# First expert pair of a mixture-of-experts encoder: its rows taken from x on chip, the experts' order formed by two small products

## What is computed

```
glog = xf @ wg_r + bg_r                    # 4 groups
g_idx = argmax(glog)
elog_g = (xf @ we_r + be_r)[group g_idx]   # 8 experts of that group
top_v, top_i = top_k(elog_g, 2)
gate = softmax(top_v) * softmax(glog)[g_idx]
for each chosen expert e of each token x:
    y += gate * ((silu(x @ w_gate[e]) * (x @ w_up[e])) @ w_down[e])
x = x + y;  out = rms_norm(x)
```

## Time and profile before

| | us |
|---|---|
| median of three runs | 1148.36 |
| span of the profiled execution | 1144.7 |
| median less that span | 3.7 |
| PE busy | 1049.2 (92%) |
| DVE busy | 463.5 (40%) |
| POOL busy | 112.9 (10%) |
| HBM over the span | 258 GB/s mean |

### The profile page before, as it was taken

How to read it: one execution, slowest core, us unless ns; L and a number is a source line. 1 busy time by engine, 2 the same in 40 slices (tenths; PEclk the granted TensorE clock), 3 DMA queues, 4 the chain that set the end, 5 groups by cost and what they waited for, 6 DMA issues and landing times.

```text
span 1144.7 us, 11623 instructions
## 1 busy us (share of the span) xinstructions
PE 1049.2 (92%) x4578; PEld 546.0 (48%) x4578; DVE 463.5 (40%) x780; ACT 186.8 (16%) x487; POOL 112.9 (10%) x169
## 2 busy tenths in 40 slices
PE   6999999999999999999999999997877789987885
PEld 3577744555444546777657433332332233333331
DVE  3259734573665025003325764332323233332235
ACT  0147133433112300112201010000000000000001
POOL 1200001132105101000000110000000000000002
PEclk9999999999999999999999899998999899999999
DMA  8611140222230733113055899999999999999997
GB/s 258 239 57 39 53 152 1 81 109 83 74 111 30 255 147 117 56 50 147 1 216 230 306 395 421 429 425 427 427 426 427 430 424 427 426 426 426 424 410 257
DMA packets 56983, 281.50 MB, mean 246 GB/s; under 512 B 13333, under 2 KB 15253, under 8 KB 44130
## 3 DMA queue, kind: packets, MB, share of 16 engines
q1 hardware_dynamic: 44882, 262.57, 57.2%
q10 hardware_dynamic: 7152, 8.96, 2.2%
q0 software_dynamic: 4896, 9.23, 2.2%
HBM read 272.82 MB, written 22.81 MB: 258 GB/s over the span
## 4 chain that ended last, share of the span: by engine, by line
PE 70%; DMA 17%; DVE 5%; SPq 5%; issue 2%; ACT 0%; DVEq 0%; POOL 0%; ACTq 0%; POOLq 0%
PE banks L517 23%; DMA arena<-in_exp_w_down_dram 14%; PE banks L505 14%; PE banks L915 10%; PE banks L905 6%; SPq L1159 4%; PE banks L521 3%; DMA arena<-expert_rows 2%; PE banks L767 2%; PE score_pair L741 2%; PE banks L655 1%; DVE arena L1769 1%; PE score_pair L571 1%; PE banks L872 1%; PE banks L605 1%
## 5 line engine op out<-in xcount | busy, mean ns | idle before, releaser
L517 PE MATMUL banks<-arena 128*128 128x512 f32 x640 | 285.6, 600 | 2.5 <-DMA arena<-in_w_in_dram 1.8
L915 PE MATMUL banks<-arena 128*64 128x512 f32 x1024 | 236.1, 617 | 36.9 <-issue 34.8
L517 PEld LDWEIGHTS banks<-arena 128*128 128x128 f32 x640 | 120.0, 192 | 147.2 <-issue 145.7
L915 PEld LDWEIGHTS banks<-arena 128*64 128x64 f32 x1024 | 83.2, 142 | 186.1 <-issue 184.8
L505 PE MATMUL banks<-arena 128*128 128x288 f32 x640 | 156.1, 406 | 0.0
L905 PE MATMUL banks<-arena 128*64 128x512 f32 x512 | 116.4, 608 | 23.8 <-DMA arena<-in_exp_w_down_dram 15.9
L505 PEld LDWEIGHTS banks<-arena 128*128 128x128 f32 x640 | 121.4, 190 | 33.8 <-issue 0.4
L1384 ACT ACTIVATE arena<-banks 128x512 f32<-128x512 f32 (+6 forms) x135 | 61.6, 492 | 377.3 <-PE banks L517 111.0
L905 PEld LDWEIGHTS banks<-arena 128*64 128x64 f32 x512 | 38.2, 140 | 90.8 <-issue 76.3
L1607 ACT ACTIVATE arena<-banks,arena 128x512 f32<-128x512 f32 x17 | 11.7, 687 | 411.4 <-PE banks L915 387.7
L2159 DVE SCALAR_TENSOR_TENSOR arena<-banks,arena 128x512 f32<-128x512 f32 x34 | 25.4, 750 | 102.8 <-PE banks L905 95.2
(11 more groups left out here) (320 smaller groups left out, 965.1 us busy)
## 6 DMA issues: line engine op xcount, KB each, us to landing
arena<-in_exp_w_gate_dram SPq DMA_DIRECT2D x30, 2048.0 KB, 32.3
arena<-in_exp_w_up_dram SPq DMA_DIRECT2D x29, 2048.0 KB, 32.9
arena<-in_exp_w_down_dram SPq DMA_DIRECT2D x28, 2048.0 KB, 35.3
arena<-in_w_in_dram SPq DMA_DIRECT2D x7, 2048.0 KB, 8.5
arena<-in_exp_w_down_dram SPq DMA_DIRECT2D x16, 512.0 KB, 11.1
expert_rows<-arena SPq DMA_DIRECT2D x4, 1152.0 KB, 8.0
out_dram<-arena SPq DMA_DIRECT2D x4, 1024.0 KB, 10.5
arena<-in_w_mem_k_dram SPq DMA_DIRECT2D x2, 2048.0 KB, 9.7
```

The lines of the kernel that those rows point to most:

```text
L517: ins = mm(b[:, :], x, w[:, k, :], start=k == 0, stop=k == KC - 1)
L915: ins = mm(bank[own, :], xgT[:, k, own], w[j][:, k, :], start=k == 0, stop=k == KC - 1)
```

## The change

Pass 0 no longer takes its rows from the gather. While tiles 3 and 4 are still being chosen, PE multiplies x (which is still in SBUF) by the one-hots of pass 0: per tile eight matmuls of 128 x 128 (`first_rows`), accumulated over the five tiles in the two banks `pair`. The result is already transposed. DVE copies it with the gain into a new buffer xgT0. These 40 matmuls replace `keep_running` (9 matmuls of 128 x 512) and pass 0's `turn_rows`.

The list product for tiles 3 and 4 (`last_near_tokens`) moves into the gate product of pass 0, before its fifth step; the read of the lists by DVE, and so both gathers, move behind DVE's whole list arithmetic. The up product of pass 0 waits until DVE has read the list, since both use banks[1]. Gather 0 is still made, because ACT and DVE need the rows of x for the sum, and ACT now waits for it.

The experts' order was a comparison of 32 x 32 in every partition, a product and a sum, three DVE operations of 1024 elements. It is now two small products on PE: one that turns the positions into a column (L896 of the kernel after), one that sums (L901, between the first and second step of the gate product), with two short DVE operations.

The late half of slot 9 waits for the first tile's `first_rows` instead of the gather.

```diff
@@ PE
             pe.wait_ge(near_hot, 2)
-            near_list = A.open(pe)[:, 0:4]
+            near_list = banks[1][:, 0:4]
+            def first_rows(t, half):
+                rows = TILES[t][1]
+                x = x_sb[0:rows, t, :].rearrange("p (d k) -> p k d", k=KC)
+                for k in range(4 * half, 4 * half + 4):
+                    ins = mm(pair[:, half, (k % 4) * P:(k % 4 + 1) * P], x[:, k, :], near_hots[0:rows, t, 0, :],
+                             start=t == 0 and k % 4 == 0, stop=t == SAMPLE, skip_group_check=True)
+                return ins
             near_tokens(0, 3)
-            pe.wait_ge(a_free, A.filled)
-            keep_running(3)
+            pe.wait_ge(lg_read, NT)
+            for t in range(2):
+                for half in range(2):
+                    ins = first_rows(t, half)
+                if t == 0:
+                    ins.then_inc(x_placed, 1)
             pe.wait_ge(sel_ready, 3)
             ranks(3, NT)
+            for half in range(2):
+                first_rows(2, half)
             pe.wait_ge(near_hot, 3)
-            near_tokens(3, NT).then_inc(near_full, 1)
-            pe.wait_ge(a_free, A.filled)
-            keep_running(6)
+            for half in range(2):
+                first_rows(3, half)
+                first_rows(SAMPLE, half).then_inc(SP_.tx_full, 1)
             pe.wait_ge(v_free, V.filled)
             pe.wait_ge(a_free, A.filled)
+            pe.wait_ge(order_in, 1)
+            mm(banks[2][0:NE, 0:1], pos[0:1, :], ones[0:1, 0:1], start=True, stop=True).then_inc(order_out, 1)
...
+                    if k == 1 and quarter_read is not None:
+                        order_sums()
+                    if k == 4 and quarter_read is not None:
+                        last_near_tokens()
...
-            pe.wait_ge(xg_ld[0], 16)
-            turn_rows(SP_, xg_rows[0])
...
+                    if i == 0:
+                        pe.wait_ge(near_std, 1)
@@ SP
-            sp.wait_ge(xg_ld[0], 16)
+            sp.wait_ge(x_placed, 1)
@@ ACT
                     act.wait_ge(table_ready, 1)
+                    act.wait_ge(xg_ld[0], 16)
@@ DVE
             near_rows(3, NT)
-            ve.wait_ge(near_full, 1)
-            listed = A.banks[mark["near"]][:, 0:4].rearrange("p (i v) -> p v i", v=2)
-            ts(near_row, listed[:, 0], float(NOROW), None, ALU.add).then_inc(near_ready, 1)
...
-            copy_rows(SP_, 0)
-            n.link(tt(order_cmp, pos.unsqueeze(1).broadcast_to([P, NE, NE]), wide(iota32, NE), ALU.is_equal))
-            n.link(tt(order_cmp, order_cmp, per_tile(iota32, NE), ALU.mult))
-            n.link(red(tmp32, order_cmp, AX_X, ALU.add))
-            v.tensor_copy(order_i, tmp32).then_inc(order_ready, 1)
+            copy_half(SP_, 0, 0, xgT0)
+            ve.wait_ge(order_out, 1)
+            ts(tmp32[0:NE, :], iota32[0:NE, :], banks[2][0:NE, 0:1], tokv[0:NE, 0:1], ALU.is_equal, ALU.mult).then_inc(order_in, 1)
+            copy_half(SP_, 0, 1, xgT0)
+            ve.wait_ge(order_out, 2)
+            ts(order_i[0:1, :], banks[2][0:1, NE:2 * NE], float(NOROW), None, ALU.add).then_inc(order_ready, 1)
...
+            ve.wait_ge(near_full, 1)
+            listed = banks[1][:, 0:4].rearrange("p (i v) -> p v i", v=2)
+            ts(near_row, listed[:, 0], float(NOROW), None, ALU.add).then_inc(near_ready, 1)
```

More of the change, by code:

```diff
@@ L864, in _, with order_sums, last_near_tokens @@
             pe.wait_ge(near_hot, 2)
-            near_list = A.open(pe)[:, 0:4]
[L866 to L872, removed]
-            near_tokens(0, 3)
-            pe.wait_ge(a_free, A.filled)
-            keep_running(3)
+            near_list = banks[1][:, 0:4]
[6 more added lines that the diff above has]
+                return ins
+            near_tokens(0, 3)
+            pe.wait_ge(lg_read, NT)
[4 more added lines that the diff above has]
+                    ins.then_inc(x_placed, 1)
             pe.wait_ge(sel_ready, 3)
             ranks(3, NT)
+            for half in range(2):
+                first_rows(2, half)
             pe.wait_ge(near_hot, 3)
-            near_tokens(3, NT).then_inc(near_full, 1)
-            pe.wait_ge(a_free, A.filled)
-            keep_running(6)
+            for half in range(2):
+                first_rows(3, half)
+                first_rows(SAMPLE, half).then_inc(SP_.tx_full, 1)
             pe.wait_ge(v_free, V.filled)
             pe.wait_ge(a_free, A.filled)
+            pe.wait_ge(order_in, 1)
+            mm(banks[2][0:NE, 0:1], pos[0:1, :], ones[0:1, 0:1], start=True, stop=True).then_inc(order_out, 1)
+            def order_sums():
+                pe.wait_ge(order_in, 2)
+                mm(banks[2][0:1, NE:2 * NE], ones[0:NE, 0:1], tmp32[0:NE, :], start=True, stop=True).then_inc(order_out, 1)
+            def last_near_tokens():
+                near_tokens(3, NT).then_inc(near_full, 1)
             def turn_rows(S, rows):
@@ L2073, in _, with copy_half @@
                 n.link(tt(rk32, rk32, tmp32, ALU.add))
+            n.link(tt(pos, others, rk32, ALU.mult))
+            n.link(stt(out=pos, in0=first2[:, 0], scalar=float(2 * OVER_AFTER), in1=pos, op0=ALU.mult, op1=ALU.add))
+            stt(out=pos, in0=first2[:, 1], scalar=float(2 * OVER_AFTER + 1), in1=pos, op0=ALU.mult, op1=ALU.add).then_inc(order_in, 1)
+            ve.wait_ge(order_in, 1)
+            def copy_half(S, n, half, xT):
+                k = slice(4 * half, 4 * half + 4)
+                ve.wait_ge(S.tx_full, 2 * n + half + 1)
+                tt(xT[:, k, :], pair[:, half, :].rearrange("p (k t) -> p k t", k=4),
+                   gain_rows[:, k].unsqueeze(2).broadcast_to([P, 4, P]), ALU.mult).then_inc(S.xT_cp, 1)
             def copy_rows(S, n):
                 for half in range(2):
[L2078 to L2090 removed]
+                    copy_half(S, n, half, xgT)
+            copy_half(SP_, 0, 0, xgT0)
[4 more added lines that the diff above has]
+            ts(order_i[0:1, :], banks[2][0:1, NE:2 * NE], float(NOROW), None, ALU.add).then_inc(order_ready, 1)
             n.link(ts(pos, pos, float(CAP), None, ALU.mult))
```

25 lines of the change are left out of this document (10 added, 15 removed).

## The result

The changed kernel takes 1158.17 us (median of 4 runs, 1155.88 to 1158.85) against 1148.05 us of the kernel before (4 runs, 1147.06 to 1148.55): ratio 1.0088, 95% interval 1.0076 to 1.0100. It is slower by 0.9%. The profiled execution took 1158.85 us with a span of 1157.1, 12.4 us more than the 1144.7 before. The medians differ by 10.1 us only: the profiled execution of the changed kernel was the longest of its four, and the one of before was a short one (more on this behind the experiments).

A forecast was written before the change was run, and what follows sets the result against it. The weight stream, unbroken from about 652 us, was taken to bound the kernel. Early loads 1.2 us earlier, with slack covering PE's 0.6 us gain, gave span 1143.5, plus 3.7 around it: 1147.2 us, range 1145.2 to 1150.0.

The forecast's parts named there:

- any rival of mine: Alternatives: late gather 1149.2 to 1151.6 us (chance 0.16), clock 1148.4 (0.10), more gain 1145.6 (0.18), no effect 1148.4 (0.08).
- The 40 matmuls: `first_rows` on PE before the gate product: 1.8 us per tile at high clock, `ranks` 0.8 us late, the rest hidden.
- rival C: PE idle at 645.5 starts the gate product at half speed, losing 1.7 us there; time 1148.4; chance 0.10.
- A clock of 0.5 in the gate product: Named sign that the forecast is wrong: the gate product running at a granted clock of 0.5.
- the 0.9 saved at `turn_h`: Between up and down product: DVE reaches its hidden values earlier, so 2.6 us instead of 3.5.
- The end as a date of the stream: Kernel end equals when the weight stream runs unbroken plus fixed bytes; the change shifts it by -1.2 us.
- The new wait: PE waits 2.3 us behind the up product for gather 1, issued at 655.6 and landing at 664.1.
- Order and list product: Both small products inside pass 0's gate product lengthen it by 1.15 us, between 0.8 and 1.4.
- The order part at nothing: Removing three 1024-wide DVE operations (3.8 us) beside the gate product gains nothing; two order records on PE take 0.3 us, partly hidden.
- gate product 3.1 us earlier, all but 0.6 taken by the gather: Gate product starts at 646.75; after the wait for gather 1 the down product starts at 666.7 against 667.32.
- the 3.7 us between the profiled span and the median: Added to the forecast span of 1143.5 us as time around it, giving 1147.2.

The follow-up runs named there:

- e2: Changed kernel with first_rows taking 128 neighbouring columns of x instead of every eighth (output not the reference's): 1148.71 us, ratio 1.0007 to the kernel before.
- e5: Changed kernel with neighbouring columns, pass 0's gate and up weights and gain reordered to match, so output is the reference's: 1148.21 us, ratio 1.0004 to the kernel before.
- e1: Kernel before with unread rows of 16 matmuls of various operand strides added at its end: 1204.74 us including those rows.
- e3: Changed kernel with the list product in front of tile 3's rows and DVE reading it behind the first copy: 1156.21 us, ratio 1.0076.
- e4: Kernel before with only the experts' order changed to two small PE products in place of three 1024-wide DVE operations: 1148.22 us, ratio 1.0006.
- e6: e5 with the list product in front of tile 3's rows and its read behind the first copy: 1144.62 us, ratio 0.9976 to the kernel before.
- e7: e6 with half of tile 1's rows moved behind `ranks`: 1145.35 us, ratio 0.9979 to the kernel before.
- e8: e5 with `turn_rows` of pass 1 moved behind pass 0's down product, gathers still late: 1145.89 us, ratio 0.9983 to the kernel before.
- e9: Changed kernel with only `turn_rows` of pass 1 moved behind pass 0's down product: 1155.69 us, ratio 1.0074 to the kernel before.
- e10: e5 with the list product between steps 1 and 2 of the gate product, read by DVE ahead of the list arithmetic: 1145.12 us, ratio 0.9978.

## Why the prediction was wrong

Forecast 1147.2 in a range of 1145.2 to 1150.0; measured 1158.17, far outside, and slower than any rival of mine.

**The step that failed** is the part "*The 40 matmuls*": 1.8 us a tile, 0.8 us of delay for `ranks` and nothing for the rest. I took the price of a record from the earlier trace rows, matmuls of the same shape and type but with neighbouring words as operands, and did not look at the address pattern that the diff itself spells out. Per tile it is 4 us, not 1.8. What hung on that term then went wrong in order:

- Tiles 0 and 1 ended at 642.7, not 639.5, so the positions were ready 2.95 us later than my 645.9, at 648.85.
- The other 48 records, forecast hidden by 645.5, took until 655.5. The gate product started 8.9 us later than forecast: 3.0 from `ranks` (with the offset of 0.74), the rest from these. With neighbouring words it started at 647.10 (e2) and 646.20 (e5), against my 646.75. Less their offsets that is 1.3 us later and 0.3 us earlier than forecast; the two differ in how long the low clock lasted (6.54 and 5.44 us for the same first 32 records).
- Gate and up product took 16.85 us (655.66 to 672.51). In e2, the same instructions took 15.47; the 1.4 us are the half clock at their start. It was rival C in kind, but C saw it behind an idle moment of PE, and here it came behind matmuls that showed no idle time. A clock of 0.5 in the gate product was one of the signs that I had named for being wrong; it stood there for the first 3 us.

**The sum closes** on the date of the loads: gate product 5.8 us later than before (offset included), gate and up 2.9 longer, from there to the down product 1.45 longer (the gather's wait of 2.17 less the 0.9 saved at `turn_h`, and small change), the down product 2.5 longer: 12.7, as in SP's timeline.

**What held.** The end as a date of the stream: 12.7 us at the loads of 674.45 gave 12.4 on the span, at unchanged rates behind 700 us. Over the profiled executions of all variants but e1 it holds within 2 us:

| | loads behind pass 0's down product | span | difference |
|---|---|---|---|
| before | 674.45 | 1144.7 | 470.25 |
| after | 687.12 | 1157.1 | 469.98 |
| e2 | 677.86 | 1147.8 | 469.94 |
| e3 | 683.05 | 1154.7 | 471.65 |
| e4 | 674.79 | 1146.7 | 471.91 |
| e5 | 675.57 | 1145.8 | 470.23 |
| e6 | 672.77 | 1144.1 | 471.33 |
| e7 | 672.57 | 1144.4 | 471.83 |
| e8 | 673.05 | 1144.9 | 471.85 |
| e9 | 683.89 | 1154.1 | 470.21 |
| e10 | 674.26 | 1144.5 | 470.24 |

The differences fall in two groups, near 470.2 and 471.7, and no run shows why. Nor does the table alone tell the stream from PE, since these loads go out when PE ends the down product; that the stream runs full behind them is read from the rates.

The new wait: 2.3 us forecast, 2.17 measured in the changed kernel and 2.83 in e2. In the changed kernel this is partly luck: gather 1 was issued 9.6 us later than forecast (665.22 for 655.6) and the up product ended 10.7 us later (672.51 for 661.85), which nearly cancel. From issue to landing it took 9.4 us there and 9.7 in e2, where I had put 8.5. Order and list product: 1.15 forecast, 1.5 in e2 (15.47 less 13.95). The order part at nothing: e4.

**What else was missed.** Even with the failed term right, the forecast was 1.6 to 2 us too kind (a ratio of 0.9990 against 1.0004 in e5 and 1.0007 in e2). Its path: gate product 3.1 us earlier, all but 0.6 taken by the gather. Not counted was that PE went on at half speed for a while behind the wait: 2.8 us on e2's down product, about 1 us in e5, where it fell on the transposes. And the 3.7 us between the profiled span and the median were not what lies around a span: that is about 1.75 in every run where both are known. The other 1.95 us say that the profiled execution of before was about that much faster than its median (an estimate, since its own time is not on record). Dates of single executions are therefore worth no more than 1 to 2 us against each other; which of e5, e6, e8 and e10 is faster is read from their medians.

An example is e10, which beats e5 by 3.1 us in the median while its loads are only 1.3 us earlier. The two profiled executions differ by 1.3 us in time as well (1147.49 and 1146.22): that of e5 was 0.7 us below its median, that of e10 1.1 above.

**Open.** What makes executions of one kernel differ by 2 to 4 us; the length of the low clock ahead of the gate product is one part that the traces show. Why the down product ran part of its time at half clock in the changed kernel, e2 and e9 and not in e5, e6, e7, e8 and e10. Of the slowdown's parts (late `ranks`, late rows, half clock) each is read from the trace, and only their sum was undone, in e2.

## What to carry to other kernels

Take the price of a matmul from a row with the same strides of both operands, not only the same shape: for the stationary one the width of LDWEIGHTS in ns, 192 against 335, tells the two apart in the trace. A strided moving operand hardly shows there (207 ns, L1062 of e1), only in the time per record. Where a new operand is a view with a step of four words or more and the moving side is narrow, reorder something that is loaded anyway (here the weights' rows, e5). And when an instruction is taken off the path, look at what else was moved with it: here the gathers went back behind the list arithmetic, and PE, in order, gave back all that was gained until they, or the instruction that waits for them, were moved (e6, e8, e10).

## What the runs showed of the hardware

- fp32 matmuls of 128 x 128 against 128 columns, at full clock: 0.117 us a record with neighbouring words, 0.123 with every second, 0.238 with every fourth, 0.243 with every eighth; 0.238 with the moving operand at every eighth. No cost with 512 moving columns (0.435) or in transposes (0.119 and 0.121), one row each.
- At half clock the strided ones take 0.278 us a record (e3, 8.89 us for 32), about a tenth more than the 0.25 at full clock in the changed kernel: halving the clock changes their pace little.
- The granted clock fell to 0.50 while PE was shown 100% busy with such matmuls in two kernels, in the changed kernel at 652 us and in e3 from 648 to 658 us (to 657 such matmuls, then the gate product):

```profile
648.00:658.00 10.00, 10.00 (x37) 8.47 (x39) 2.56 (x11) 0.00 (x0) 2.31 (x2) 0.50 0.13 38
```

Contiguous ones in the same place (e2, the stretch from 640.5) kept it at 1.00:

```profile
640.50:646.60 6.10, 6.10 (x51) 5.62 (x50) 5.25 (x28) 0.32 (x2) 0.00 (x0) 1.00 0.92 391
```

But the changed kernel's strided ones, too, had run at 1.00 for 13 us before the fall (`ranks` among them):

```profile
638.50:651.60 13.10, 13.10 (x57) 12.86 (x57) 6.01 (x33) 0.32 (x2) 0.00 (x0) 1.00 0.74 314
```

And e1's strided rows L1058 to L1062 ran 23 us on end at 1.00. So the clock fell in both kernels with strided matmuls while PE was shown busy, and not in e2, which differs from the changed kernel in the stride alone; but the stride does not bring it down by itself, and what set off the fall these rows do not show.
